# One step of a hybrid decoder layer: the sample's key and value compression moved from ahead of the norm and projections into the decode stage

## What is computed

```python
def rms_norm(x, g):
    xf = x.astype(jnp.float32)
    y = xf * lax.rsqrt(jnp.mean(xf * xf, -1, keepdims=True) + EPS)
    return (y * g.astype(jnp.float32)).astype(x.dtype)
...
def compress(rows, w1, b1, w2, pe):
    B, T = rows.shape[:2]
    nch = T // CMP_STRIDE
    ch = rows[:, :nch * CMP_STRIDE].reshape(B, nch, CMP_STRIDE, N_KV, HEAD_DIM)
    first = jnp.einsum('bnjgd,jdh->bngh', ch, w1[:CMP_STRIDE])
    second = jnp.einsum('bnjgd,jdh->bngh', ch, w1[CMP_STRIDE:])
    bias = b1 + jnp.einsum('jd,jdh->h', pe, w1)
    h = jax.nn.gelu(first[:, :-1] + second[:, 1:] + bias)
    return jnp.einsum('bngh,hd->bngd', h, w2)
...
def mixer_in(x, pos, g_pre, w_in):
...
    z = rms_norm(x, g_pre) @ w_in
...
def layer_out(x, conv_y, o_nsa, w_out, g_post, g_pre2, w_up, w_down, g_post2):
    mix = jnp.concatenate([conv_y, o_nsa.astype(conv_y.dtype)], -1) @ w_out
    h = x + rms_norm(mix, g_post)
    f = jnp.square(jax.nn.relu(rms_norm(h, g_pre2) @ w_up)) @ w_down
    return h + rms_norm(f, g_post2)

```

## Time and profile before

| | us |
|---|---|
| median of three runs | 886.17 |
| profiled execution, device time | 884.8 |
| its span in the trace | 883.0 |
| TensorE matmuls busy | 789.3 |
| VectorE busy | 477.7 |
| GpSimd busy | 366.6 |
| ScalarE busy | 232.1 |
| mean granted TensorE clock, share of full | 0.949 |

### The profile page before, as it was taken

One profiled execution on the slowest core, in us unless ns is written; L12 is line 12 of the kernel. 1 busy time (PEld: TensorE's weight loads), 2 busy tenths in 40 slices (PEclk: granted clock), 3 DMA queues, 4 the chain that ended last, 5 costly groups with the idle time before them and its releaser, 6 DMA issues.

```text
span 883.0 us, 15001 instructions
## 1 busy us (share of the span) xinstructions
PE 789.3 (89%) x6261; PEld 719.8 (82%) x6261; DVE 477.7 (54%) x665; ACT 232.1 (26%) x429; POOL 366.6 (42%) x127
## 2 busy tenths in 40 slices
PE   4898999999697873999897999999999999999990
PEld 4898999998444551566796999999999999999990
DVE  3557589873488576777366953363003333322227
ACT  3354222421221134677312322230000222201020
POOL 3440400000020252000073277777777777777754
PEclk9899999999797895999999899999999999999995
DMA  8721532424861332000012122222222222222102
GB/s 330 311 110 44 210 134 91 133 84 78 187 177 38 110 126 76 1 2 1 1 49 96 48 96 95 95 96 92 79 79 87 94 96 95 95 96 95 48 0 97
DMA packets 23726, 85.42 MB, mean 97 GB/s; under 512 B 7184, under 2 KB 10816, under 8 KB 16192
## 3 DMA queue, kind: packets, MB, share of 16 engines
q1 hardware_dynamic: 9504, 57.35, 18.4%
q0 software_dynamic: 3456, 16.78, 5.7%
q10 hardware_dynamic: 10720, 10.64, 4.5%
HBM read 80.47 MB, written 8.47 MB: 101 GB/s over the span
## 4 chain that ended last, share of the span: by engine, by line
PE 78%; DVE 13%; ACT 3%; DMA 2%; issue 2%; ACTq 0%; DVEq 0%; POOL 0%; POOLq 0%
PE PA L1261 29%; PE PB L1261 29%; PE PA L1315 4%; DVE yC L1116 2%; PE PR L1291 2%; PE PR L1584 2%; PE PB L1596 1%; PE PS L1604 1%; DVE smx L1132 1%; DMA rkw<-cwk_dram 1%; PE PR L1454 1%; PE PA L1468 1%; PE PA L1432 1%; DVE yC L854 1%; PE PA L1596 1%
## 5 line engine op out<-in xcount | busy, mean ns | idle before, releaser
L356 POOL TENSOR_TENSOR wH<-wraw,zero 128x2048 fp32r<-128x2048 f32 x38 | 137.3, 3613 | 249.1 <-PE PB L1261 199.9
L359 POOL TENSOR_TENSOR wL<-wraw,wH 128x2048 fp32r<-128x2048 f32 x38 | 183.8, 4838 | 3.0
L854 DVE SCALAR_TENSOR_TENSOR yC<-uP,vec,yC 128x512 f32<-128x512 f32 (+1 forms) x135 | 83.5, 685 | 0.1
L1194 DVE TENSOR_TENSOR hL<-h,hH 128x520 f32 (+1 forms) x32 | 52.5, 1643 | 49.2 <-ACT hH L726 49.2
L1261 PE MATMUL PA<-hL,wH 128*128 128x260 f32 x256 | 72.2, 282 | 0.0
L1261 PE MATMUL PB<-hL,wH 128*128 128x260 f32 x256 | 72.2, 282 | 0.0
L1261 PE MATMUL PA<-hH,wL 128*128 128x260 f32 x256 | 72.2, 282 | 0.0
L1261 PE MATMUL PA<-hH,wH 128*128 128x260 f32 x256 | 72.2, 282 | 0.0
L1261 PE MATMUL PB<-hH,wL 128*128 128x260 f32 x256 | 72.2, 282 | 0.0
L1261 PE MATMUL PB<-hH,wH 128*128 128x260 f32 x256 | 72.2, 282 | 0.0
L398 POOL DMA_INDIRECT rks<-pool_ks_dram,idx x8 | 7.8, 972 | 149.7 <-PE PA L1412 110.6
(11 more groups left out here) (375 smaller groups left out, 2145.0 us busy)
## 6 DMA issues: line engine op xcount, KB each, us to landing
wraw<-wblk_dram SPq DMA_DIRECT2D x49, 1024.0 KB, 4.8
xT<-x_fm_dram SPq DMA_DIRECT2D x1, 2080.0 KB, 11.6
y_fm_dram<-xT SPq DMA_DIRECT2D x8, 260.0 KB
rkw<-cwk_dram ACTq DMA_DIRECT2D x8, 256.0 KB, 2.9
rkw<-cwv_dram ACTq DMA_DIRECT2D x8, 256.0 KB, 2.6
s_win_dram<-cwk_dram ACTq DMA_DIRECT2D x1, 2044.0 KB
s_win_dram<-cwv_dram ACTq DMA_DIRECT2D x1, 2044.0 KB
p_rows_dram<-ktok ACTq DMA_DIRECT2D x4, 256.0 KB, 2.2
```

What stands on the lines that cost most here:

```text
L356: pool.tensor_tensor(wH[s][:, :], wraw[s][:, :], zero[:, :].broadcast_to([P, BW]), ALU.add)\
L359: pool.tensor_tensor(wL[s][:, :], wraw[s][:, :], wH[s][:, :].bitcast(F32), ALU.subtract)\
L854: dve.scalar_tensor_tensor(out=dst, in0=src, scalar=w, in1=first, op0=ALU.mult, op1=ALU.add)\
L1194: dve.tensor_tensor(lo, h2[c % 2][:, :], hi.bitcast(F32), ALU.subtract).then_inc(s_hl, 1)
```

## The change

The order of stages becomes: norm and projection, gates, prompt compression and prompt scores, then the key stage with the sample compression woven in, then the value products.

- **Start.** x is loaded in four pieces ahead of the weight blocks. Six of its eight squares are made by ScalarE and two by VectorE, each in a buffer of its own (`psq`); TensorE adds all eight by matmuls with ones. Root, reciprocal and the normalised halves follow, and the first two projection groups run k by k behind them (`first_groups`).
- **Weight blocks.** Blocks 2, 3, 11, 12, 13 and 14 are split by ScalarE and VectorE and no longer by GpSimd. The compression's weights are those that the prompt's compression loads (blocks 11 and 12), so two loads fall away.
- **Prompt compression** runs over 66 columns; two of them carry the position rows, from which the bias comes.
- **Woven units.** `cmp_mm(u)` calls `between(u, jp)` after each of eight steps. Units 0 to 3 carry the transposes of unit u+1, and `turn_keys` and `key_scores` of samples 2u and 2u+1; units 4 to 7 carry the transposes, the compressed scores, block selection, the transposes of probabilities, and the convolution's means. The three thirds of `turn_keys` go through one bank, `PS[:, 0]`. The unit's sum stands in bank 1 or 0 of `PB` (`ACC_BANK`).
- **Memory.** The raw pages (two buffers) lie where x lay, and x is loaded again for the residual. `XL` lies over `wraw`, so blocks 13 and 14 load after the last unit.
- **Value pages** go into four buffers, two of them in `KTb`. Window loads and the stores of the convolution's state move from ScalarE's queue to SyncE's.
- **Tail.** The transposes of `od` stand inside the second pair's step, and the rounding of blocks 13 and 14 inside the convolution's layer norm.

The core of the diff:

```diff
-NORM_AT = {5: (0, 1), 6: (2, 3, 4), 7: (5, 6, 7)}
+XU = 2052
+ACC_BANK = (1, 1, 1, 1, 1, 0, 1, 0)
...
+        xr = region([("xT", [P, KT, T], F32)], [("rawc0", [P, 2048], F32), ("rawc1", [P, 2048], F32)])
+        xT, rawc = xr["xT"], [xr["rawc0"], xr["rawc1"]]
+        wr = region([("wraw0", [P, BW], F32), ("wraw1", [P, BW], F32)], [("XL", [P, 2, XU], F32R)])
+        wraw, XL = [wr["wraw0"], wr["wraw1"]], wr["XL"]
...
+        psq = [zr0, zr1, zr2, t1, t2, kf0, kf1, sg]
...
+        vsel = [rks[0], rks[1], KTb0[:, 0:1024], KTb1[:, 0:1024]]
+        vwin = [rkw[0], rkw[1], KTb0[:, 1024:1536], KTb1[:, 1024:1536]]
```

SyncE and GpSimd (loads):

```diff
+            def load_x(i):
+                sp.dma_start(xT[:, 2 * i:2 * i + 2, :], A["x_fm"][:, 2 * i:2 * i + 2, :]).then_inc(s_x[i], 16)
+            load_x(0)
+            load_x(1)
+            sp.dma_start(wraw[0][:, :], A_wblk[B_IN]).then_inc(s_raw[0], 16)
+            load_x(2)
+            load_x(3)
             sp.dma_start(vec[:, :], A["vecs"]).then_inc(s_vec, 16)
-            sp.dma_start(ident[:, :], A["consts"][:, 0:P]).then_inc(s_vec, 16)
...
+            sp.wait_ge(s_gmm, 1)
+            key_window(0)
+            key_window(1)
+            for b in range(2, NS):
+                sp.wait_ge(s_kt, 3 * (b - 1))
+                key_window(b)
...
+            sp.wait_ge(s_cmm, 8)
+            load(1, 13)
+            load(0, 14)
+            for b in range(4, NS):
+                sp.wait_ge(s_dpv, b - 3)
+                value_window(b)
+            sp.wait_ge(s_xt, 32)
+            sp.dma_start(xT[:, :, :], A["x_fm"]).then_inc(s_x2, 16)
...
-                dec_load(i)
-            split(13, 1, 16 * 7, 5, s_grp, 16)
-            split(14, 0, 16 * 8, 6, s_grp, 18)
-            split(15, 1, 16 * 8, 7, s_grp, 20)
-            split(16, 0, 16 * 9, 8, s_grp, 22)
...
+            key_load(0)
+            key_load(1)
+            gather(2)
+            for u in range(3):
+                key_load(2 * u + 2)
+                key_load(2 * u + 3)
+                gather(u + 3)
+            value_load(0)
+            value_load(1)
+            gather(6)
+            value_load(2)
+            value_load(3)
+            gather(7)
+            for b in range(4, NS):
+                value_load(b)
```

ScalarE:

```diff
+            load_table(ACT.Sqrt)
+            for k in (0, 1, 2, 3, 4, 6):
+                act.wait_ge(s_x[k // 2], 16)
+                if k == 4:
+                    block_hi(B_IN)
+                act.activation(psq[k][:, :], xT[:, k, :], ACT.Square).then_inc(s_sq0, 1)
+            root(0, PB)
+            for k in range(KT):
+                act.wait_ge(s_nt, k + 1)
+                act.activation(actH[k], sq[k % 2][:, :], ACT.Copy).then_inc(s_nh, 1)
+                if k == 3:
+                    block_hi(B_IN + 1)
...
+                act.activation(KTb[b % 2][:, 512 * q:512 * q + 512], PS[:, 0, :], ACT.Copy).then_inc(s_ktA, 1)
+            for i in range(4):
+                x_evac(0, i)
+            for u in range(4):
+                for e in range(2):
+                    key_evac(2 * u + e, 0)
+                    x_evac(u + 1, 2 * e)
+                    key_evac(2 * u + e, 2)
+                    x_evac(u + 1, 2 * e + 1)
+                gelu(u)
...
+            for i in range(4):
+                x_evac(6, i)
             act.wait_ge(s_dV, DV_SMAX)
             act.activation(Ss[:, 0:PAST + 1], Ss[:, 0:PAST + 1], ACT.Exp, bias=dsm[:, 8:9], accum_out=dsm[:, 9:10])\
                 .then_inc(s_dA, 1)
             act.wait_ge(s_dV, DV_WMAX)
             act.activation(Sw[:, 0:WIN + 1], Sw[:, 0:WIN + 1], ACT.Exp, bias=dsm[:, 4:5], accum_out=dsm[:, 5:6])\
                 .then_inc(s_dA, 1)
-            act.wait_ge(s_dP, DP_PTS)
-            act.activation(PT[:, 0:512], PR[:, 0, :], ACT.Copy).then_inc(s_dA, 1)
             act.wait_ge(s_cV, 3)
             act.activation(Pc, Pc, ACT.Exp).then_inc(s_cX, 1)
-            for i in range(NS + 2, NS + 5):
-                window_load(i)
-            for t in range(CT):
+            gelu(5)
...
                 act.activation(sq[t % 2][:, :], yC[:, t, :], ACT.Square).then_inc(s_ta, 1)
+            square_conv(0)
+            square_conv(1)
+            gelu(6)
+            square_conv(2)
+            square_conv(3)
+            act.wait_ge(s_dP, DP_PTS)
+            act.activation(PT[:, 0:512], PR[:, 0, :], ACT.Copy).then_inc(s_dA, 1)
+            gelu(7)
```

VectorE:

```diff
+                dve.wait_ge(s_x[k // 2], 16)
+                dve.tensor_tensor(psq[k][:, :], xT[:, k, :], xT[:, k, :], ALU.mult).then_inc(s_sq0d, 1)
+            block_lo(B_IN)
+            dve.wait_ge(s_vec, 16)
+            rinv(0)
+            for k in range(KT):
+                if k >= 2:
+                    dve.wait_ge(s_nl, k - 1)
+                dve.scalar_tensor_tensor(out=sq[k % 2][:, :], in0=xT[:, k, :], scalar=vec[:, V_GPRE + k:V_GPRE + k + 1],
+                                         in1=rb[:, :], op0=ALU.mult, op1=ALU.mult).then_inc(s_nt, 1)
+                if k >= 1:
+                    norm_lo(k - 1)
...
+            for u in range(4):
+                x_lo(u + 1, 0)
+                key_evac(2 * u)
+                conv_some(3)
+                x_lo(u + 1, 1)
+                if u == 0:
+                    cv(dve.tensor_reduce(cmx, p3, AX.X, ALU.max))
+                    cv(dve.tensor_tensor(p3, p3, cmx.unsqueeze(2).broadcast_to([P, 32, 32]), ALU.subtract))
+                if u >= 1:
+                    cmp_out_evac(u - 1)
+                conv_some(3)
+                x_lo(u + 1, 2)
+                key_evac(2 * u + 1)
+                conv_some(3)
+                x_lo(u + 1, 3)
...
+            x_lo(6, 2)
+            x_lo(6, 3)
             dve.wait_ge(s_sc, NS)
...
+            x_lo(7, 0)
+            cmp_out_evac(5)
+            x_lo(7, 1)
```

TensorE:

```diff
+            def turn_keys(b, q):
+                if q == 0:
+                    pe.wait_ge(s_dec[b % 2], 16 * (b // 2 + 1))
+                    pe.wait_ge(s_win[b % 2], 16 * (b // 2 + 1))
...
+                        pe.wait_ge(s_ktA, 2 * b)
+                elif q == 1:
+                    pe.wait_ge(s_ktA, 2 * b + 1)
+                else:
+                    pe.wait_ge(s_ktD, b + 1)
                 for r in range(4):
-                    mm = pe.transpose(PS[:, 0, r * P:(r + 1) * P], rkw[b % 2][:, r * P:(r + 1) * P], ident[:, :])
+                    src = rkw[b % 2][:, r * P:(r + 1) * P] if q == 2 else rks[b % 2][:, (4 * q + r) * P:(4 * q + r + 1) * P]
+                    mm = pe.transpose(PS[:, 0, r * P:(r + 1) * P], src, ident[:, :])
...
+            def between(u, jp):
+                if jp == 1 and u >= 1:
+                    cmp_out(u - 1)
+                if u < 4:
+                    if jp == 4:
+                        key_scores(2 * u)
+                    if jp % 4 == 0:
+                        turn_keys(2 * u + jp // 4, 0)
+                if jp % 2 == 1 and u < 7:
+                    turn(u + 1, jp // 2)
+                if u < 4 and jp % 4 in (1, 2):
+                    turn_keys(2 * u + jp // 4, jp % 4)
+                if u < 4 and jp == 7:
+                    key_scores(2 * u + 1)
+                if (u, jp) == (4, 3):
+                    cmp_scores()
+                if (u, jp) == (4, 7):
+                    pe.wait_ge(s_dV, DV_PN)
+                    pe.transpose(PS[0:64, 1, 64:128], Sc0[:, :], ident[0:64, 0:64]).then_inc(s_dP, 1)
+                if (u, jp) == (5, 0):
+                    pe.wait_ge(s_dV, DV_PN + 1)
+                    pe.matmul(PS[0:64, 1, 128:144], pnT[:, :], C(C_OV, 16, 0, 64), start=True, stop=True)\
+                        .then_inc(s_dP, 1)
+                if (u, jp) == (5, 3):
+                    pe.wait_ge(s_dV, DV_PN + 2)
+                    pe.wait_ge(s_w2e, 5)
+                    pe.matmul(PS[0:64, 1, 144:160], C(C_RS, 64, 0, 64), im1[:, :], start=True, stop=True)\
+                        .then_inc(s_dP, 1)
+                if (u, jp) == (6, 4):
+                    mean_conv()
+                if (u, jp) == (7, 2):
+                    square_means(0)
+                    square_means(1)
+                if (u, jp) == (7, 4):
+                    turn_probs()
+                if (u, jp) == (7, 6):
+                    square_means(2)
+                    square_means(3)
...
+                acc = PB[:, ACC_BANK[u], 0:256]
+                for jp in range(8):
+                    if jp % 2 == 0:
+                        pe.wait_ge(s_xl, 4 * u + min(jp // 2 + 2, 4))
+                    for sh in range(2):
+                        t = jp + 8 * sh
+                        w = slice(t * P, (t + 1) * P)
+                        x = slice(256 * jp + sh, 256 * jp + sh + 256)
+                        for i, (W_, X_) in enumerate(((wH, XH), (wH, XL), (wL, XH))):
+                            mm = pe.matmul(acc, W_[s][:, w], X_[:, u % 2, x], start=(t == 0 and i == 0),
+                                           stop=(t == 15 and i == 2), skip_group_check=True)
```

(3 more changed lines are left out.)

941 lines of the change are left out of this document (442 added, 499 removed).

## The result

The changed kernel takes 873.46 us (median of 4; 868.62 to 874.50), the kernel before 886.56 beside it (4; 885.34 to 887.61): a ratio of 0.984 [0.980, 0.988], 13.1 us less. The sign is the forecast one and the time lies in the range, but the gain is under half of the 30 us that the sum promised. The profiled execution took 874.44 with a span of 872.3, against 884.8 and 883.0.

| step | before | after | change | forecast |
|---|---|---|---|---|
| start to group 2 of the projection | 102.56 | 37.16 | -65.4 | -66.2 |
| group 2 to the end of the gates | 108.84 | 116.44 | +7.6 | 0 |
| prompt's compression and scores | 15.16 | 19.45 | +4.3 | +1.0 |
| woven stage (before: keys and softmax) | 59.22 | 132.15 | +72.9 | +65.6 |
| value products and tail, to the pairs | 60.16 | 29.32 | -30.8 | -30.6 |

What follows compares the result with a forecast made beforehand. TensorE sets the end, so only stages where it waits can shorten. Terms -66.2 + 1.0 + 65.6 - 30.6 = -30.2 us, from the median 886.17 to 856.0; forecast 847 to 866 (0.62), range 846 to 876 (0.83).

Steps and rivals of the forecast that it cites:

- the front: Start to projection group 2: compression leaves, the norm stands alone; group 2 starts at 36.4 for 102.56, -66.2 us.
- The in-projection and gates stay as they are: Projection from group 2 to the gates' end: length unchanged, 0 us; the gates' end moves from 211.40 to 145.2.
- Moved queues: Window loads on SP's queue, page gathers on GpSimd's: no cost, or 1 to 3 us if two gathers meet a late one.
- Rival 4: Front: x slow or block 5 late behind window copies; group 2 at 45, 862 to 868 us; chance 0.21 with rival 2.
- I take half of it, 3.6, on a warm PE: Prompt's 32 score matmuls, moved ahead of the weave: half of the earlier 7.06 us; the window grows by 1.0.
- units 0 to 3: Weave with key pages: 15.8 us PE work a unit, two open waits of 1.0 each; 17.85 a unit, 71.4 for four.
- Units 4 to 7: Weave with the selection chain: 10.85, 10.7, 19.0 (7.5 wait, 3.0 half clock) and 12.8 us, together 53.4.
- value products and tail: Stage ahead of the pairs: 60.2 to 29.6 us, by four buffers, covered tail and GpSimd no longer splitting blocks 13, 14; -30.6.
- Rival 1: Weave tighter: evacuations always early, units of 16 us, unit 6 with 3 us of wait; 835 to 846 us; chance 0.08.
- Rival 3: Many short waits drop the clock to half through the whole weave: +75 us, some 930, slower than before; chance 0.05.
- the row: Profile of the kernel before: clock 1.00 over 20 us of key pages with short waits, so the weave keeps it outside unit 6.
- rivals 2 and 4: Looser weave (thirds wait for both queues, 22 us a unit, 866 to 876) or late front (862 to 868); together 0.21.

Runs made afterwards that it cites:

- key-copy experiment: Changed kernel with VectorE evacuating a key page's second third ahead of the rounding x_lo in units 0 to 3; 867.02 us, 0.9795 of the kernel before.
- gelu(5) experiment: Changed kernel with unit 5's gelu ahead of the three exponentials on ScalarE, not behind them; 869.03 us, 0.9800 of the kernel before.

## Why the prediction was right and wrong, step by step

**Right: the front.** Reciprocal from 16.77 (forecast 15.5), first two groups cold from 22.52, group 2 at 37.16 (36.4). No step is off by more than 1.3.

**Failed: "The in-projection and gates stay as they are", +7.6.** I carried the stage over as a fixed length because PE was busy for all of it. But it was busy with little to spare: the window copies ran beside it before as well, and block 5 was ready 5.4 us ahead of its use. The move brought the copies nearer to that load and set two gathers beside both, and the load grew from 17.5 us to 26.7. "Moved queues" asked only which transfers the change moves, and allowed "1 to 3 us if two gathers meet a late one"; the copies, which no line of the diff moves, were in no sum. Rival 4 named the right event (block 5 late behind the window copies) but placed it ahead of group 2, where the trace has it ahead of group 6. Two experiments settle it: without the copies block 5 takes 9.3 us and PE does not wait, without the gathers 23.7 and PE waits 2.5. How much of the 9.2 is the nearness of the copies alone was not separated.

**Failed: "I take half of it, 3.6, on a warm PE", +3.3.** The size was right for a warm PE, 3.76 in two experiments. That PE would be warm was the unsupported part: `kcBD` stands on VectorE behind two roundings, PE idles 1.68 us, and the scores take 6.25. Rows 8 had shown the same 32 matmuls at 7.06 behind an idle of 1.06 (the granted clock there was 0.50 from 274.8 on); the higher end was the row at hand.

**Mis-sized: units 0 to 3, "15.8 of PE work" and "1.0 each", +4.5.** Work is 17.1, waits are eight of 0.8. The work term failed by 1.3 a unit, the wait term by 0.4 the other way, and unit 0 had the cold clock of the step above on top, 1.6 by its difference from the other three; at 20.18 it is just over the 20 us that I had named as a sign of being wrong. The 1.3 lies in the compression matmuls, 7.2 where I had 5.76 (starts in the key-copy experiment): that term was taken from a row of 12 matmuls behind each other, and the weave breaks them into runs of six, each with a longer first and last step.

**Units 4 to 7, +2.8.** Unit 4 is 10.99 (10.85), unit 6 is 17.82 (19.0) with its wait of 7.07 (7.5) at the place named: the costliest wait of the weave was right in cause and size, and the gelu(5) experiment confirms it. Unit 5 was 12.14 or 10.57 (10.7), with and without a fall of the clock. Unit 7 is 15.26 (12.8), mis-sized: behind its wait for gelu(6), 2.2 us, the clock fell again, which I had charged only in unit 6. By its first eight sums of squares (3.43 us at 0.50, the next eight 1.92) that is about 1.5 of the 2.5; the rest was not separated.

**Right: value products and tail, -30.6** (-30.8). The cause given, VectorE slowed while GpSimd splits blocks, holds; but the gain is tied to who splits, as three experiments show, and not to the order of the tail. 18.5 of the 30.8 is the tail behind the value products; the other 12.4 are the value products themselves (41.68 before, 29.32 now), and their cause, four buffers for two, was not tested by itself.

**Rivals.** Rival 1 (a tighter weave) fell: units of 18.6. Rival 3 (half clock through the weave) fell: 1.00 in units 1 to 3, with eight waits of 0.7 to 0.9 us in the weave. The rule that I had set against the row, of the Trainium skill, page "TensorE: Matmul & The Clock Gate", section "A second HAM failure mode: psum-queue depth-cycling", lets the clock swing under short idles between groups of matmuls. The trace has such a fall behind single idles of 1.6 to 7.1 us, at five places from group 2 on, two of which (1.61 and 1.68) keep 1.00 in some profiles, and none behind those of 0.7 to 0.9. Of rivals 2 and 4 the time came true, 866 to 876, by another mix: units at 18.6, not 22, and a late block.

## What to carry to other kernels

A stage that is moved meets the transfers of its new time: list for it also the transfers that the diff does not touch, with their bytes, set them beside the loads it needs, and note how long ahead of its use each load landed before. Before charging a matmul at its warm price, look at the wait ahead of it. Where an operation is slow because of its neighbour, ask who does the neighbour's work after the change; delaying it only moves the cost.
